# Last attention: VectorE makes the high and low parts of the rotated queries and keys

## The reference

```
q = rms_norm(q, qn_g)
k = rms_norm(k, kn_g)
q = concat([q[..., :128], rope(q[..., 128:], cos, sin)])
k = concat([k[..., :128], rope(k[..., 128:], cos, sin)])
s = q @ k.T * scale          # blocks of 128 queries against all keys up to the block's end
p = softmax(where(mask, s, -inf))
o = p @ v
out = x + (o * silu(z)) @ w_out
```

## Time and profile before

| | us |
|---|---|
| median of 3 runs (1772.65 to 1774.3) | 1773.58 |
| the profiled execution | 1772.31 |
| its span, first to last instruction | 1770.2 |

### The profile page before, as it was taken

How to read it: one execution, slowest core, us unless ns; L and a number is a source line. 1 busy time by engine, 2 the same in 40 slices (tenths; PEclk the granted TensorE clock), 3 DMA queues, 4 the chain that set the end, 5 groups by cost and what they waited for, 6 DMA issues and landing times.

```text
span 1770.2 us, 21748 instructions
## 1 busy us (share of the span) xinstructions
PE 1696.3 (96%) x8565; PEld 1229.0 (69%) x8565; DVE 854.5 (48%) x1578; ACT 644.1 (36%) x1110; POOL 96.1 (5%) x131
## 2 busy tenths in 40 slices
PE   6999999999989799999999998999999999999899
PEld 5888888888868644344343433788788888988677
DVE  3544345555654523333333334871647643447782
ACT  4122225555541311111111123655353222557860
POOL 0000001001000000000000000110010000000320
PEclk9999999999999799999999999999999999999999
DMA  7666364663136669999999995233023342313101
GB/s 151 89 107 96 107 84 83 66 75 75 49 131 262 248 284 425 428 426 426 428 426 427 426 427 221 90 113 95 25 79 100 95 157 79 105 54 97 49 1 72
DMA packets 111349, 317.54 MB, mean 179 GB/s; under 512 B 6485, under 2 KB 79957, under 8 KB 98448
## 3 DMA queue, kind: packets, MB, share of 16 engines
q1 hardware_dynamic: 108080, 309.57, 53.0%
q0 software_dynamic: 2160, 3.92, 0.6%
q10 hardware_dynamic: 1008, 2.65, 0.4%
HBM read 313.78 MB, written 6.30 MB: 181 GB/s over the span
## 4 chain that ended last, share of the span: by engine, by line
PE 89%; DMA 3%; DVE 3%; ACT 3%; issue 1%; SPq 0%; DVEq 0%; ACTq 0%; POOL 0%; POOLq 0%
PE bank L1420 15%; PE bank L1422 15%; PE bank L1421 15%; PE bank L1736 11%; PE bank L1762 6%; PE turned L1420 4%; PE turned L1422 4%; PE turned L1421 4%; DMA up<-in_w_e_up 2%; PE bank L1501 2%; PE turned L1501 1%; PE bank L1804 1%; PE bank L1611 1%; PE bank L1749 1%; DMA w_raw<-in_w_in 1%
## 5 line engine op out<-in xcount | busy, mean ns | idle before, releaser
L2054 DVE TENSOR_TENSOR w_lo<-w_raw,w_hi 128x2048 fp32r<-128x2048 f32 (+1 forms) x72 | 156.9, 2180 | 283.7 <-ACT w_hi L902 283.6
L902 ACT ACTIVATE w_hi<-w_raw 128x512 fp32r<-128x512 f32 (+3 forms) x138 | 169.8, 1253 | 289.7 <-DMA w_raw<-in_w_in 101.6
L1736 PE MATMUL bank<-gate,xt 128*64 128x512 f32 x512 | 225.8, 594 | 1.1 <-DMA up<-in_w_e_up 1.1
L1737 PE MATMUL bank<-up,xt 128*64 128x512 f32 x512 | 225.8, 594 | 0.0
L1736 PEld LDWEIGHTS bank<-gate,xt 128*64 128x64 f32 x512 | 68.7, 137 | 139.6 <-issue 139.6
L1420 PE MATMUL bank<-h1T_hi,w_hi 128*128 128x512 f32 x376 | 150.9, 401 | 0.0
L1422 PE MATMUL bank<-h1T_hi,w_lo 128*128 128x512 f32 x376 | 147.1, 391 | 0.0
L1421 PE MATMUL bank<-h1T_lo,w_hi 128*128 128x512 f32 x376 | 146.6, 390 | 0.0
L1762 PE MATMUL bank<-down,hT 128*64 128x512 f32 x256 | 118.4, 606 | 8.8 <-DVE hT L2387 8.8
L902 ACT ACTIVATE y_s<-bank,slot_w 64x512 f32<-64x512 f32 x63 | 43.0, 683 | 220.6 <-PE bank L1763 99.5
L1763 PE MATMUL bank<-down,hT 128*64 128x512 f32 x256 | 118.4, 606 | 0.0
(11 more groups left out here) (703 smaller groups left out, 3821.4 us busy)
## 6 DMA issues: line engine op xcount, KB each, us to landing
down<-in_w_e_down SPq DMA_DIRECT2D x32, 2048.0 KB, 24.4
up<-in_w_e_up SPq DMA_DIRECT2D x30, 2048.0 KB, 26.6
gate<-in_w_e_gate SPq DMA_DIRECT2D x30, 2048.0 KB, 21.8
w_raw<-in_w_in SPq DMA_DIRECT2D x24, 1024.0 KB, 9.5
w_raw<-in_a_w_in SPq DMA_DIRECT2D x20, 1024.0 KB, 5.3
w_raw<-in_w_in SPq DMA_DIRECT2D x16, 512.0 KB, 10.7
w_raw<-in_a_w_out SPq DMA_DIRECT2D x8, 1024.0 KB, 5.1
w_raw<-in_w_conv_out SPq DMA_DIRECT2D x4, 1024.0 KB, 5.4
```

The lines of the kernel that those rows point to most:

```text
L902: return nc.scalar.activation(out, in_, ACT.Copy, scale=scale)
L1736: g_ins = pe.matmul(out[0:CAP, :], x, ring_gate[p][:, c, :], start=c == 0, stop=c == KC - 1)
L1737: u_ins = pe.matmul(out[CAP:, :], x, ring_up[p][:, c, :], start=c == 0, stop=c == KC - 1)
L2054: V.tensor_tensor(ring_view(w_lo, n), ring_view(raw, n), ring_view(w_hi, n).bitcast(F32), ALU.subtract)\
```

## The change

The four instructions for each head leave GpSimd's list and stand in VectorE's, with the same waits. Those of head 0 come ahead of VectorE's attention loop, those of head h+1 in `among3`, behind the maximum and bias of the second item of head h (i mod 4 = 1) and ahead of a key step or a piece of the split at the same item.

```diff
@@ gpsimd @@
-            for h in range(CH):
-                p, own, other = h % 2, half_rows(h % 2), half_rows(1 - h % 2)
-                if h >= 2:
-                    pool.wait_ge(results, order[("S3", TT * (h - 2) + TT - 1)] + 1)
...
-                until_taken(pool, ("qpT", h // 2))
-                step(nc.gpsimd.tensor_copy(rope_q[p][own, :], qpT[own, h // 2, :]))
-                nc.gpsimd.tensor_tensor(rope_q[p][other, :], qpT[own, h // 2, :], rope_q[p][own, :].bitcast(F32), ALU.subtract)
-                pool.wait_ge(sem("rope_k_made"), h + 1)
-                step(nc.gpsimd.tensor_tensor(rope_k_lo[p][own, :], kpT[own, h // 2, :], rope_k[p][own, :].bitcast(F32), ALU.subtract))
-                nc.gpsimd.tensor_copy(rope_k_lo[p][other, :], rope_k_lo[p][own, :]).then_inc(sem("rope_split"), 1)
@@ vector @@
+            def rope_parts(h):
+
+                p, own, other = h % 2, half_rows(h % 2), half_rows(1 - h % 2)
+                if h >= 2:
+                    dve.wait_ge(results, order[("S3", TT * (h - 2) + TT - 1)] + 1)
+                elif h == 1:
+                    dve.wait_ge(results, order[("ukv", 3, TT - 1)] + 1)
+                else:
+                    dve.wait_ge(sem("q_roped"), 1)
+                until_taken(dve, ("qpT", h // 2))
+                step(V.tensor_copy(rope_q[p][own, :], qpT[own, h // 2, :]))
+                V.tensor_tensor(rope_q[p][other, :], qpT[own, h // 2, :], rope_q[p][own, :].bitcast(F32), ALU.subtract)
+                dve.wait_ge(sem("rope_k_made"), h + 1)
+                step(V.tensor_tensor(rope_k_lo[p][own, :], kpT[own, h // 2, :], rope_k[p][own, :].bitcast(F32), ALU.subtract))
+                V.tensor_copy(rope_k_lo[p][other, :], rope_k_lo[p][own, :]).then_inc(sem("rope_split"), 1)
+
+            rope_parts(0)
+
             def among3(i):
+                if i % TT == 1 and i // TT + 1 < CH:
+                    rope_parts(i // TT + 1)
                 if i == 2:
                     key_squares(3)
```

## The result

The changed kernel takes 1777.53 us (median of 7 runs, 1776.76 to 1781.75), the kernel before beside it 1772.65 us (7 runs, 1771.15 to 1774.3). The ratio is 1.0029 with a 95% interval of 1.0020 to 1.0039: slower by 4.9 us. The profiled execution took 1777.7 us with a span of 1775.7 us, 5.5 us longer than before.

The account below looks back on a forecast made before the run. The prediction saw TensorE and VectorE nearly full (7.31 and 7.32 of 7.6 us a head), with VectorE becoming the bound in heads 3 to 6. It forecast 1773.58 + 2.0 = 1775.6 us, range 1772.4 to 1779.0.

Parts of the forecast that it names:

- the slower rival: Opening, `var` of `key_squares(3)`: its 0.6 us slack is gone, root, loads and exponential of item 3 shift; 1778.0 us, chance 0.25.
- two signs of being wrong: PT(7) to PT(11) already late, or TensorE's waits in heads 3 to 5 below 1 us in all.
- the walk: The prediction's step-by-step timing of the engines through the opening (heads 0 to 2) and the middle (heads 3 to 5).
- The lock's end: Without GpSimd work here all biases take 0.16 us; `kr` is no longer stretched, and ScalarE passes on 0.4 us.
- The opening: Heads 0 to 2: delays from rope parts are covered, `turn_k(3)` starts at 1669.5, TensorE 1.4 us ahead.
- the step of the cover: Opening: rope parts 0 end at 1650.1; ScalarE's table load, at 1651.3, just covers the later bias at about 1651.2.
- The middle: Heads 3 to 5: VectorE becomes the bound with 24.3 us of work from item 13; PT(23) comes 2.0 us later.
- the three satisfied waits: Waits in the rope parts for old scores, evicted `qpT` and ScalarE's `rope_k`: taken as nothing, of 0 to 0.1 us each.
- three places of new waits: Middle heads: TensorE newly waits at O(4h+3), for a copy behind rope parts, and at PT(4h+2) and PT(4h+3).
- The first rival: Three-item lag takes in the rope parts; middle waits and the opening's 1.4 us come back: -3.0 us, 1770.6, chance 0.10.
- The end: Heads 6 and 7: the lag holds the difference, so the 2.0 us stay to the output projection's first transpose.
- What bounds the kernel before: TensorE and VectorE nearly full; some 0.4 us per middle head is TensorE waiting for an exponential behind a stretched bias.

Follow-up runs that it names:

- e5: The kernel before with the bias made by tensor_scalar (one tensor, one per-partition scalar) in place of tensor_tensor: 1773.86 us, ratio 1.0005.
- e7: The kernel before, GpSimd starting parts 2 to 7 behind the bias of the fourth item, not behind its scores: 1775.33 us, ratio 1.0006.
- e1: The changed kernel with rope parts 0 moved ahead of the last sum of squares of the slices: 1774.55 us, ratio 1.001.
- e6: The changed kernel with rope parts 0 early and the weight-split pieces spread to later items: 1773.56 us, ratio 1.0005.
- e9: The changed kernel with parts 0 early, parts 4 to 7 back on GpSimd, started by the bias of the fourth item: 1770.89 us, ratio 0.9985.
- e10: The changed kernel with parts 0 early, parts 4 to 7 back on GpSimd, started by the old wait on scores: 1770.61 us, ratio 0.999.
- e2: The changed kernel with rope parts 4, 5 and 6 back on GpSimd with the old waits: 1771.16 us, ratio 0.9995.
- e3: The changed kernel with the first cast of rope parts 4, 5 and 6 made twice: 1777.79 us, ratio 1.0028.
- e4: The changed kernel with the eight weight-split pieces at items 11, 15, 19, 23, 27, 29, 30, 31: 1775.06 us, ratio 1.0011.
- e11: As e10, with the weight-split pieces at items 11, 15, 19, 23, 27, 29, 30, 31: 1769.36 us, ratio 0.9978 against the kernel before.

## Why the prediction was right and wrong

**Direction and mechanism: right, size: less than half.** The median came 4.9 us later where 2.0 were forecast. The 1777.53 us lie above the forecast's own band (1774.5 to 1777.1) and near the slower rival's 1778.0, which had a chance of 0.25. That they are only 1.9 us from 1775.6 is in part luck: the kernel before, timed beside it, took 0.9 us less than the 1773.58 that the sum starts from. Of the prediction's two signs of being wrong the first came true: PT(7) came at 1673.39 (before 1672.34) and PT(11) at 1680.41 (before 1679.63), so the opening failed. The second did not: TensorE's waits in heads 3 to 5 are 4.2 us by the records.

PT(23) came 5.1 us later, counted from a place that both executions share (next paragraph). The 3.1 us over the forecast's 2.0 are 2.05 in the opening (26.65 by the walk, where S(13) at 1678.15 puts PT(11) at about 1677.95; 28.70 measured) and 1.15 in the middle (26.2 and 27.35), less 0.1 ahead of the load.

**The lock's end: right.** All biases take 0.16 us, and TensorE no longer waits for `kr` at slice 3. The 0.4 us that this was to bring at the load came, as 0.52. Both loads stand at 1651.71, but executions reach this stage at different times, so the gain has to be counted from a place ahead of the lock. Timeline of VectorE, `var` of slice 2, of before, then of after.

```profile
1637.27 0.18 DVE L2813 TENSOR_SCALAR var<-ssq 128x16 f32<-128x16 f32 x1
```

```profile
1637.79 0.18 DVE L2798 TENSOR_SCALAR var<-ssq 128x16 f32<-128x16 f32 x1
```

From there to the load it is 14.44 us before and 13.92 after. The other kernels agree: 14.43 and 14.44 in e5 and e7, where GpSimd works beside `kr`, and 13.91 to 13.93 in all the rest. No code ahead of `var` differs, so the 0.52 us by which the execution of after was late there are taken as the difference between executions.

**The opening: wrong, and it was the step of the cover.** I had rope parts 0 end at 1650.1, and the load of ScalarE at 1651.3 to cover it. Timeline of VectorE, of after: the first and last of rope parts 0, the bias of item 1 and the first of rope parts 1, the maximum of item 2, `var`.

```profile
1648.55 0.42 DVE L2859 CAST rope_q<-qpT 64x512 fp32r<-64x512 f32 x1
...
1650.42 0.42 DVE L2863 CAST rope_k_lo<-rope_k_lo 64x512 fp32r<-64x512 f32 x1
...
1652.98 0.16 DVE L2846 TENSOR_TENSOR nb<-neg_max,rq 128x1 f32<-128x1 f32 x1
1653.17 0.42 DVE L2859 CAST rope_q<-qpT 64x512 fp32r<-64x512 f32 x1
...
1655.40 0.55 DVE L2845 TENSOR_REDUCE neg_max<-bank 128x1 f32<-128x384 f32 x1
...
1657.51 0.18 DVE L2798 TENSOR_SCALAR var<-ssq 128x16 f32<-128x16 f32 x1
```

Timeline of ScalarE, of after: the load, the exponential of item 2, the load ahead of the root, the exponential of item 3.

```profile
1651.71 1.28 ACT L1054 ACT_TABLE_LOAD   x1
...
1656.18 0.67 ACT L1054 ACTIVATE p_t<-bank,nb,rq 128x384 f32<-128x384 f32 x1 [0.96 <-DVE nb L2846]
...
1658.12 1.28 ACT L921 ACT_TABLE_LOAD   x1
...
1660.94 0.78 ACT L1054 ACTIVATE p_t<-bank,nb,rq 128x512 f32<-128x512 f32 x1
```

Rope parts 0 started 0.55 us later than I had them and took 2.29 us, so they ended 0.7 later; 0.52 of the 0.55 are the late execution. Counted from the load, parts 0 ended 0.87 us ahead of it where the walk had 1.2, and parts 1 started 1.46 us behind it where the walk had 0.8; they pushed the maximum of item 2 to 1655.40. I had looked at the cover of `var` behind that maximum and had not put a time on the exponential of item 2, which ScalarE does ahead of the load: it waits 0.96 us for the bias, and the load ahead of the root starts at 1658.12 in place of 1657.04. This is the slower rival with its chain, but not with its first link: `var`, written at 1657.51, was still covered, since the root takes it at 1659.41. The chain broke one instruction earlier than I had it. The rival named rope parts of 2.4 us as the point from which it decides; 2.29 us were enough, because the biases of items 0 and 1 came later behind parts 0 than in the walk (the second ends 2.3 us behind them, the walk had 2.0), and the 0.6 us of slack were no margin for a walk whose marks were off by as much. The gain behind it was sized rightly: with rope parts 0 out of the way (e1) the opening takes 26.56 us, and the walk had 26.65.

Then the clock added its part. Windows of before and of after in the opening (columns as in the earlier trace rows; the third number from the end is the granted clock, as a share of 2.4 GHz).

```profile
1655.00:1675.00 20.00, 15.01 (x102) 12.62 (x101) 16.05 (x44) 14.22 (x33) 7.65 (x8) 0.91 0.01 2
...
1663.50:1667.50 4.00, 4.00 (x27) 2.92 (x27) 3.16 (x9) 1.97 (x5) 0.89 (x2) 0.99 0.01 2
```

```profile
1655.00:1675.00 20.00, 15.83 (x93) 12.81 (x92) 17.29 (x52) 13.41 (x32) 0.00 (x0) 0.83 0.01 1
...
1663.50:1667.50 4.00, 4.00 (x15) 3.09 (x15) 3.62 (x9) 1.04 (x3) 0.00 (x0) 0.50 0.02 4
```

TensorE waited 3.35 us for the exponential of item 3 and then ran at half of 2.4 GHz for 6.8 us (1661.0 to about 1667.8), before for 3.4 us. A mean clock of 0.83 in place of 0.91 over 20 us is, as an estimate, 1.6 us of work at full speed. From PT(3) to `turn_k(3)` it was 10.18 us before, 1.63 of them the wait for `kr`, and 10.16 after without a wait, which agrees. So up to `turn_k(3)`: 1.08 of later exponential, 1.6 of clock, less the 1.63 us that TensorE no longer waits for `kr`, gives 1.05, and it came at 1672.02, 1.05 later. I had it 1.4 earlier. The kernels with the exponential at 8.15 or 8.16 us behind the load (before, e1, e5, e6, e9, e10) have 0.91 in that window; after, e2, e3 and e4, with it at 9.23 to 9.25, have 0.83. What doubles the slow stretch is only argued from these pairs. e7 (8.15, and 0.80) and e11 (9.01, and 0.95) don't fit a rule on the exponential alone; that stays open. e11 and e10 have the same code up to item 11, and TensorE waits 1.78 and 1.77 us for the first exponential. In e11 the clock then fell, from about 1653.4 to 1656.9, the scores of item 3 and with them exp(3) came late, and it didn't fall again; in e10 it fell only behind the wait for exp(3). So where the clock falls isn't fixed by the kernel, and some 0.85 us of an opening can come from that alone.

**The middle: right in path and kind, 1.15 us short.** Timeline of VectorE, of after, rope parts 4 and the piece of splitting behind them.

```profile
1681.30 0.42 DVE L2859 CAST rope_q<-qpT 64x512 fp32r<-64x512 f32 x1
1681.76 0.69 DVE L2860 TENSOR_TENSOR rope_q<-qpT,rope_q 64x512 fp32r<-64x512 f32 x1
1682.46 0.68 DVE L2862 TENSOR_TENSOR rope_k_lo<-kpT,rope_k 64x512 fp32r<-64x512 f32 x1
1683.18 0.42 DVE L2863 CAST rope_k_lo<-rope_k_lo 64x512 fp32r<-64x512 f32 x1
1683.63 0.69 DVE L2044 TENSOR_TENSOR w_lo<-w_raw,w_hi 128x512 fp32r<-128x512 f32 x1
```

The four start steps are 0.46, 0.70, 0.72 and 0.45: 2.33 us against the 2.12 of the prediction. The term that was mis-sized is the pitch of the second and of the fourth instruction: 0.70 where I had 0.60, and 0.45 where I had 0.34. I had granted the three satisfied waits nothing, and that seems right: the copy of PT at 1684.24 waits for TensorE and starts 0.61 behind the piece in front of it. Timeline of VectorE, of after: the last cast of parts 2 and the copy behind it, then the same of parts 3.

```profile
1664.08 0.42 DVE L2863 CAST rope_k_lo<-rope_k_lo 64x512 fp32r<-64x512 f32 x1
1664.53 0.69 DVE L2236 COPY pT_t<-bank 128x512 f32<-128x512 f32 x1
```

```profile
1674.87 0.42 DVE L2863 CAST rope_k_lo<-rope_k_lo 64x512 fp32r<-64x512 f32 x1
1675.21 0.68 DVE L2236 COPY pT_t<-bank 128x512 f32<-128x512 f32 x1
```

The copies have the same waits, and the pitch is 0.45 and 0.34. What differs is the half of the partitions: the last cast of an even head writes 64 to 127, that of an odd head 0 to 63, and the copy writes from 0 on. The first cast of an odd head, which works on 64 to 127, starts 0.19 us behind the start of the bias in front of it, that of an even head 0.07 to 0.08. So the longer pitch goes with a change of the half. It changes between the second and the third instruction of every head; ahead of the piece behind parts 5, where only the half that is read changes, the pitch is 0.45 too. No run varies that alone, so as a cause it isn't shown. Three parts by 0.21 are 0.6 of the 1.15 us; the rest of VectorE's list to the bias of item 23 was 0.25 longer, its start 0.17 later, and from that bias to PT(23) it is 1.77 us where 1.65 were worked out.

The three places of new waits were named rightly: O(15) and O(19) wait 0.82 and 0.83 us for VectorE's copy, PT(15), PT(19) and PT(23) 0.54 to 0.67 for an exponential, and PT(14), PT(18) and PT(22) 0.22 each. The first rival (the lag takes in the rope parts) fell with them, and with e3.

**The end: right.** 16.77 us from PT(23) to the output projection, before 16.78.

**What bounds the kernel before: one step read wrongly.** The 0.4 us of wait in each middle head I put down to the stretched bias and the exponential behind it, as if these two were the path. At item 19 the exponential does wait for its bias (0.51 us); at item 23 it waits for nothing, and the chain starts at the bias of item 22 (e5). e5 showed that without any stretched bias the middle doesn't fall: 22.95, against 22.51. The rule (the Trainium skill, SBUF — State Buffer, Who interferes with whom) holds in the form of the trace, 0.74 us against 0.16, but what it costs is VectorE's time. Had I priced it so, the gain of the change would have been the same 0.58 us a head against 2.33 us of work, which settles it without any path.

## What to carry to other kernels

Before moving work between two engines that share a lock, add up for each engine what it has to do in one turn of the loop: here 0.6 us of lock were traded for 2.3 us of work on an engine at 7.3 of 7.6 us. Move what falls in turns with room, leave the rest, and spread fillers (the weight split) over the turns that stay below the bound; that version (e11) was the fastest. When a walk says that a chain is covered by 0.6 us, list every instruction of that chain with its time, the small ones too, and count the rival in which it isn't covered for as much as the forecast.

## What the runs showed of the hardware

- A bias of 128x1 made from a tensor and a scalar for each partition took 212 to 215 ns in 32 of 32 cases, 15 of which started while a GpSimd instruction ran (e5); the form with two tensor inputs took up to 1275 ns. The lock then falls on the next instruction with two inputs in SBUF (1.68 us for a 128x512 subtraction of pitch 0.60).
- GpSimd pays too: its 64x512 cast took 1.01 us when VectorE's work lay beside it (e7).
- On VectorE the next instruction started 0.70 us behind a subtraction of 512 columns, in place of 0.60, and 0.45 us behind a cast of 0.42, in place of 0.34, where the half of the partitions changed between the two. Satisfied waits for other engines added nothing (0.61 us, and 0.34).
- In one window of 20 us the mean granted clock was 0.80 to 0.95 in kernels that do nearly the same matmuls there; the slow stretch behind TensorE's idle place was 3.4 us in one and 6.8 us in another, and in e11 it lay from about 1653.4 to 1656.9, ahead of where e10, with the same code up to item 11, has it.
- From one profiled execution to the next this stage began up to 5.9 us earlier or later; the stretch from `var` of slice 2 to the load repeated within 0.02 us among kernels with the same work there.
